# First projection group of layer 0: order of the high parts, two low parts on GpSimd, and the second token tile begun inside the first

## The reference, cut to what matters

```python
def rms_norm(x, g):
    x32 = x.astype(jnp.float32)
    y = x32 * lax.rsqrt(jnp.mean(x32 * x32, axis=-1, keepdims=True) + EPS)
    return (y * g.astype(jnp.float32)).astype(x.dtype)

def mixer_sublayer(x, cos, sin, norm_pre, w_in, ...):
    h = rms_norm(x, norm_pre)
    z = h @ w_in          # then attention, convolution and pooling on slices of z
    ...

def reference(x, ...):
    h = x
    for l in range(DEPTH):            # 2 layers
        h = h + mixer_sublayer(h, ...)
        h = h + ffn_sublayer(h, ...)  # rms_norm, silu(h @ w_gate) * (h @ w_up), @ w_down, rms_norm
    return h
```

## Time and profile before

| what | value |
|---|---|
| median of three runs | 794.12 us |
| the profiled execution's own time | 794.23 us |
| its span, first to last instruction | 792.4 us |
| TensorE busy | 784.0 us (99%) |
| VectorE busy | 567.6 us (72%) |
| ScalarE busy | 427.6 us (54%) |
| GpSimd busy | 78.2 us (10%) |
| mean granted TensorE clock | 0.999 |

### The profile page before, as it was taken

The page is one execution under the profiler, slowest core; times in us unless marked ns, Lnnn a source line. Parts: engine busy times, 40 slices in busy tenths (PEclk is TensorE's granted clock), DMA queues, the critical chain, the costliest instruction groups (busy, mean ns, idle before and its releaser), DMA issues.

```text
span 792.4 us, 10213 instructions
## 1 busy us (share of the span) xinstructions
PE 784.0 (99%) x3740; PEld 661.7 (84%) x3740; DVE 567.6 (72%) x814; ACT 427.6 (54%) x604; POOL 78.2 (10%) x111
## 2 busy tenths in 40 slices
PE   8999999999999999999999999999999999999997
PEld 7998888888888888888889888888888888888885
DVE  6688999879675666654476979996896755556553
ACT  6577565564564454454475666556545545445441
POOL 1620000113210000000221100002203000000000
PEclk9999999999999999999999999999999999999999
DMA  9675444536567666676355654444564676666641
GB/s 357 225 247 164 156 160 134 185 125 192 171 234 229 215 210 207 210 249 208 130 201 170 223 176 133 145 150 160 166 213 167 228 223 210 226 208 213 208 156 54
DMA packets 51729, 151.26 MB, mean 191 GB/s; under 512 B 9776, under 2 KB 14896, under 8 KB 51680
## 3 DMA queue, kind: packets, MB, share of 16 engines
q1 hardware_dynamic: 51280, 148.93, 56.6%
q0 software_dynamic: 256, 1.16, 0.4%
q10 hardware_dynamic: 144, 0.52, 0.2%
HBM read 143.77 MB, written 1.05 MB: 183 GB/s over the span
## 4 chain that ended last, share of the span: by engine, by line
PE 98%; DMA 1%; ACT 0%; DVE 0%; DVEq 0%; POOLq 0%; issue 0%; SPq 0%; POOL 0%; ACTq 0%
PE acc L438 28%; PE acc L440 28%; PE acc L439 28%; PE acc L557 7%; PE tp L512 3%; PE misc L719 1%; PE tp L737 1%; PE tp L524 1%; DMA gates<-x_cols 1%; PE misc L679 0%; PE tp L695 0%; PE misc L439 0%; PE misc L438 0%; PE misc L440 0%; PE misc L681 0%; ACT w_hi L858 0%
## 5 line engine op out<-in xcount | busy, mean ns | idle before, releaser
L1189 DVE TENSOR_TENSOR w_lo<-raw,w_hi 128x1024 fp32r<-128x1024 f32 (+2 forms) x246 | 299.1, 1227 | 128.3 <-ACT w_hi L858 127.6
L858 ACT ACTIVATE w_hi<-raw 128x1024 fp32r<-128x1024 f32 (+2 forms) x252 | 258.6, 1039 | 167.6 <-PE acc L440 161.1
L438 PE MATMUL acc<-w_hi,xT_hi 128*128 128x512 f32 (+2 forms) x692 | 268.2, 388 | 0.0
L440 PE MATMUL acc<-w_hi,xT_lo 128*128 128x512 f32 (+2 forms) x692 | 264.9, 383 | 0.0
L439 PE MATMUL acc<-w_lo,xT_hi 128*128 128x512 f32 (+2 forms) x692 | 264.7, 383 | 0.0
L440 PEld LDWEIGHTS acc<-w_hi,xT_lo 128*128 128x128 f32 x692 | 129.9, 188 | 24.8
L439 PEld LDWEIGHTS acc<-w_lo,xT_hi 128*128 128x128 f32 x692 | 130.0, 188 | 23.9
L438 PEld LDWEIGHTS acc<-w_hi,xT_hi 128*128 128x128 f32 x692 | 130.0, 188 | 23.6
L438 PE MATMUL acc<-w_hi,hT_hi 128*128 128x512 f32 (+1 forms) x300 | 117.3, 391 | 0.0
L440 PE MATMUL acc<-w_hi,hT_lo 128*128 128x512 f32 (+1 forms) x300 | 116.2, 387 | 0.0
L439 PE MATMUL acc<-w_lo,hT_hi 128*128 128x512 f32 (+1 forms) x300 | 116.1, 387 | 0.0
(11 more groups left out here) (147 smaller groups left out, 638.9 us busy)
## 6 DMA issues: line engine op xcount, KB each, us to landing
raw<-weights SPq DMA_DIRECT2D x247, 512.0 KB, 3.7
raw<-weights SPq DMA_DIRECT2D x14, 384.0 KB, 3.8
gates<-gates SPq DMA_DIRECT2D x160, 32.0 KB, 2.5
raw<-weights SPq DMA_DIRECT2D x8, 288.0 KB, 4.1
gain<-gains SPq DMA_DIRECT2D x4, 512.0 KB, 6.4
x_sb<-x_rows SPq DMA_DIRECT2D x2, 512.0 KB, 9.5
out_rows<-x_sb SPq DMA_DIRECT2D x4, 256.0 KB, 2.0
const<-consts POOLq DMA_DIRECT2D x1, 896.0 KB, 7.9
```

The lines of the kernel that those rows point to most:

```text
L438: pe.matmul(out, a_hi, b_hi, start=start, stop=False)
L440: return pe.matmul(out, a_lo, b_hi, start=False, stop=stop)
L858: ins = act.activation(w_hi[:, s, first:end], raw[:, s, first:end], ACT.Copy, scale=by)
L1189: ins = dve.tensor_tensor(w_lo[:, s, 0:width], raw[:, s, 0:width], f(w_hi[:, s, 0:width]), ALU.subtract)
```

## The change

In the first group of layer 0 three orders change, and two low parts change engine.

- ScalarE makes the high parts in the order X0, units 0 and 1, X1, units 2 and 3, X2, X3, unit 4.
- GpSimd makes the low parts of units 1 and 3, ahead of its wait for five high parts.
- VectorE's order is: scale X0, scale X1, low X0, low of unit 0, low X1, low of unit 2, scale X2, scale X3, and on as before.
- TensorE's order for tile 0: high and low x of unit 0, high and low x of unit 1, low weight 0, high 2, low x 2, low weight 1, high 3, low x 3, low weight 2, then two pairs of tile 1 (high 0 and high 1), then low weight 3, which ends tile 0. Tile 1 goes on without the two pairs that are already done.

The number of matmuls stays the same. The loops of layer 1 keep their orders.

```diff
-POOL_LO |= {(l, u) for l in range(1, LAYERS) for u in (0, 1)}
+POOL_LO |= {(l, u) for l in range(1, LAYERS) for u in (0, 1)} | {(0, 1), (0, 3)}
...
+                    def high(i, t):
+                        if i < 4 and i % 2 == 0:
+                            pe.wait_ge(tp_hi, hi0 + 2 * t + i // 2)
+                        if t == 0:
+                            pe.wait_ge(hi_done, base + u0 + i + 1)
+                        return products(i, t, xT_hi, w_hi)
...
+                        if given and t == 0:
+
+
+                            for i in range(2):
+                                high(i, t)
+                                low_x(i, t, False)
+                            low_w(0, t, False)
+                            high(2, t)
+                            low_x(2, t, False)
+                            low_w(1, t, False)
+                            high(3, t)
+                            low_x(3, t, False)
+                            low_w(2, t, False)
+                            for i in range(2):
+                                high(i, 1)
+                            low_w(3, t, True).then_inc(full[0], 1)
+                            continue
...
+                            if not given or i > 1:
+                                high(i, t)
+                            low_w(i, t, False)
+                            mm = low_x(i, t, True)
...
                     for h in range(2):
                         hi_scaled(f"X{h}", xT_hi[:, 4 * h:4 * h + 4, tokens(0)])
-                    his(0, 4)
+                        his(2 * h, 2 * h + 2)
...
-                    los(0, 4)
+                    for h in range(2):
+                        scaled(f"X{h}", 4, P, C_PRE + 4 * h)
+                    for h in range(2):
+                        k = slice(4 * h, 4 * h + 4)
+                        lo_T(f"X{h}", xT_lo[:, k, tokens(0)], xT_hi[:, k, tokens(0)])
+                        los(2 * h, 2 * h + 1)
                     x_parts("X", 1, C_PRE)
...
                 if l == 0:
+                    lo(1)
+                    lo(3)
                     pool.wait_ge(hi_done, 5)
```

More of the change, by code:

```diff
@@ L531, in first_group, with products @@
                     hi0 = l * len(HI_OF) + HI_OF.index(f"{name}0") + 1
+                    def products(i, t, src, w, last=False):
+                        s, b = (base + u0 + i) % RING, acc[:, 2 * (i // 4) + t, :]
+                        for j in range(2):
+                            kt = 2 * i % KD + j
+                            mm = pe.matmul(b, src[:, kt, tokens(t)], w[:, s, 512 * j:512 * (j + 1)],
+                                           start=kt == 0 and src is xT_hi and w is w_hi,
+                                           stop=last and kt == KD - 1)
+                        return mm
@@ new lines, in high, with low_x @@
+                    def high(i, t):
[4 more added lines that the diff above has]
+                        return products(i, t, xT_hi, w_hi)
+                    def low_x(i, t, last):
+                        if i < 4 and i % 2 == 0:
+                            tp_emptied(pe, l, TPN[f"{name}{2 * t + i // 2}"])
+                        return products(i, t, xT_lo, w_hi, last)
@@ L532, in first_group, with low_w @@
+                    def low_w(i, t, last):
+                        if t == 0:
+                            unit_ready(u0 + i)
+                        return products(i, t, xT_hi, w_lo, last)
                     for t in range(TOK):
                         bank_free(t, use)
+                        if given and t == 0:
[13 more added lines that the diff above has]
+                            continue
@@ L534, in first_group @@
                         for i in range(4 if given else 5):
-                            s, h, b = (base + u0 + i) % RING, 2 * t + i // 2, acc[:, 2 * (i // 4) + t, :]
-                            kts = [(j, 2 * i % KD + j) for j in range(2)]
                             if i == 4:
@@ L1270, in _ @@
                     post_norm(l - 1, 0, 1)
-                x_parts("X", 0, C_PRE)
-                if l:
+                    x_parts("X", 0, C_PRE)
                     los(0, 4)
```

## The result

The changed kernel is slower. Its six runs gave 796.43, 796.69, 798.24, 798.25, 798.31 and 798.37 us, median 798.25 us, against 794.08 us (793.93 to 794.16) for the kernel before. The ratio on record is 1.0045, 95% interval 1.0033 to 1.0058; the two medians alone would give 1.0053. The forecast was 796.5 us, range 795.2 to 797.7. Two runs are where it put them, and four are 1.8 us above. So there are two things to explain: the 2.4 us that every run has, and the 1.8 us that most have.

The account below looks back on a forecast made before the run. TensorE was taken to set the pace, so the second group's delay moves the end: -0.83 - 0.49 + 3.31 + 0.43 = +2.42 us. Forecast 794.12 + 2.4 = 796.5 us, range 795.2 to 797.7.

Parts of the forecast that it names:

- TensorE's chain and its slack: Whole run: TensorE sets the pace, so the end moves as much as the second group's start at 20.05 us.
- cover for the later units: Units after the first group: loads and high parts stay in time, put at nothing; a miss adds up to 0.5 us.
- The gain at the start: Layer 0's first matmul: it starts 0.83 us earlier, as unit 0's high part ends at 7.66 instead of 8.49.
- The turns: Layer 0's start: VectorE and GpSimd each wait for the other's whole instruction; TensorE then idles 3.31 us in three waits.
- The shorter handover of the earlier trace: At 184 us: an instruction that waited ends 0.13 us sooner after release than its free duration says, 1.22 to 1.08.
- the small instruction of the earlier trace: Dispatched at 26.93 us, it ends 0.11 us after VectorE's; taken to agree with the skill's "DVE-end + ~115 ns".
- the prediction's estimate: Layer 0's four handovers: each at 0.115 us plus the full duration would make the sum about +3.4; not adopted.
- Sum: Second group's start: -0.83 earlier start, -0.49 old losses, +3.31 idles, +0.43 slow first pairs, together +2.42 us.
- Rival 1: Layer 0's start: VectorE and GpSimd do not block each other; -1.08 us, giving 793.0 us; chance 0.09.
- Rivals 2 and 3: Layer 0's start: 2, VectorE keeps GpSimd out, +1.5 us, chance 0.08; 3, low X1 passes first, +2.8 us, chance 0.08.
- Rival 4: First group: TensorE's clock falls from the three pauses; half pace over ten pairs adds 4.6 us, 801 us; chance 0.03.

Follow-up runs that it names:

- pool_memset: The changed kernel with GpSimd writing zeros into the low parts of units 1 and 3 in layer 0 instead of subtracting: median 793.09 us, ratio 0.9987.
- pool_alone: The kernel before, with only the low parts of units 1 and 3 moved to GpSimd and the other engines' orders kept: median 796.39 us, ratio 1.0028.
- dve_both: The changed kernel with the low parts of units 1 and 3 back on VectorE, new ScalarE and TensorE orders kept: median 794.38 us, ratio 1.0005.
- after_look: The changed kernel with no edit, one execution, run for a profile of a slower execution: 798.18 us, clock 0.997.

## Why the prediction was right, and where it was not

- **TensorE's chain and its slack.** Right: no new wait behind the first group in any profile, and the next group's start explains the time to within 0.3 us (22.42, 22.13, 21.32, 20.29 and 19.05 us go with 796.4, 796.4, 795.5, 794.4 and 793.3 us, without the clock's share; before, 20.05 with 794.1). VectorE, ScalarE and SyncE had cover for the later units, which was put at nothing.
- **The gain at the start.** 0.83 us expected, 0.79 measured (7.85 for 8.64).
- **The turns.** Right in order and size. Ends expected at 11.20, 11.75, 14.02 and 15.10; measured 11.22, 11.77, 14.02 and 15.10. The shorter handover of the earlier trace rows held. The prediction was wrong to take the small instruction of the earlier trace rows as a case of another one: it ends 0.11 us behind VectorE's, and takes 0.25 us alone, so it too ends 0.14 us sooner than its release plus its free duration. The "DVE-end + ~115 ns" of the Trainium skill (SBUF — State Buffer, A bandwidth-pool intuition that's wrong) is given there for a DMA that waits for GpSimd's descriptors. Read as the prediction's estimate has it, as 0.115 us plus the full duration, it would have made the sum 3.4, and no handover here agrees with that. The Trainium skill (SBUF — State Buffer, Who interferes with whom) says that a GpSimd instruction that only writes does not contend with a VectorE instruction with two inputs in SBUF; pool_memset's rows agree (0.69 us beside a zeroing).
- **Sum.** Next group 2.42 us later expected, 2.37 measured. pool_alone and dve_both divide it: +2.3 for GpSimd's part alone, +0.4 for the reorder alone, and together less than their sum, since both end in the same pause for X2.
- **Rival 1** (no blocking) fell as a description of this kernel. Its price of 793.0 was near what the kernel gives when nothing blocks: pool_memset, with shorter work on GpSimd, gave 793.09. **Rivals 2 and 3** fell: GpSimd came in at 8.97 and 11.77, before VectorE's next instruction each time. Each time GpSimd had also asked first (8.81 for 9.21, 11.20 for 11.70), so whether the order of asking decides or the engines simply alternate, no run here tells.
- **Rival 4, the clock, is the step that failed.** The sum has no term for the clock; it was left to this rival, with a chance of 0.03 and a price of 4.6 us. The clock falls in 8 of 12 executions and costs about 1.8 us (1.6 of them seen in after_look's pairs), which put the median (798.25) over the upper end of the range (797.7). The argument against it was that one pause of 1.61 us had left the pace at 0.455. That is one pause. The change has pauses of 1.0 and 1.4 us and a third of 0.7, counted from where the next pair could have started, with only five pairs in between. The price was too high since the clock came back after some 4 us: the loss fell on four pairs and not on ten. The single forecast stood for one of two outcomes, and the less frequent one: that two runs lie on 796.5 confirms the turns, and not the time that this kernel mostly takes.

## What to carry to other kernels

Before an elementwise operation is moved to GpSimd to relieve VectorE, look at where the second input of VectorE's instructions lies at that moment. If both inputs are in SBUF, the two engines take turns by whole instructions, and since GpSimd takes twice as long (2.40 for 1.22 us here), the pair is slower than VectorE alone. In this kernel GpSimd's work cost VectorE nothing beside instructions with an input in PSUM, or when it did not read (pool_memset). And count pauses of TensorE not by their own length alone: several of a microsecond close together can bring its clock down in some executions, so time such a kernel in many runs and look at the clock of each.

## What was not expected of the hardware

- Counting a pause from where the next pair could have started, the granted clock fell behind three of 1.0, 1.4 and 0.7 us in 8 of 12 executions, and perhaps behind a single one of some 2.2 us in 3 of 11 (by their times alone: no profile caught one of these three). No run shows it in 11 with one of 1.1 us, in 8 with three of 0.7, 0.5 and 0.6, or in 6 with the three filled. These counts are from two chips. What sets the odds within one kernel stays open. One thing that differs is how the warm-up went: its 32 records take 6.22 us in the upper group's one profile, and 5.63 and 5.38 in the lower group's two. But pool_alone's profile has 6.26 and kept its clock, so this alone does not decide it.
- A blocked instruction ends 0.13 to 0.15 us sooner behind its release than its free duration says. The prediction had this from two sizes; it holds on both engines and for free durations of 0.25, 0.68, 1.22, 1.29 and 2.40 us (0.11, 0.55, 1.08, 1.15 and 2.25 us behind the release). So some fixed part seems to run while it is blocked; which part, no trace shows.
